# A combined high/low stationary operand for the 64-row sample tile in a feed-forward down projection

## The reference, cut to what matters

```python
h2 = _rms(x, P['norm_ffn_pre'])
u = jnp.square(jax.nn.relu(jnp.einsum('btd,df->btf', h2, P['w_up'])))      # 1024 -> 4096
x = x + _rms(jnp.einsum('btf,fd->btd', u, P['w_down']), P['norm_ffn_post'])  # 4096 -> 1024
```

## Time and profile before

| | |
|---|---|
| median of three runs | 2052.18 us (2047.31 to 2055.45) |
| profiled execution | 2048.07 us |
| its span in the trace | 2046.5 us |
| TensorE busy with matmuls | 1841.5 us, 90% |
| VectorE / ScalarE / GpSimd busy | 819.1 / 614.0 / 396.6 us |
| mean granted TensorE clock | 0.913 |

### The profile page before, as it was taken

The page is one execution under the profiler, slowest core; times in us unless marked ns, Lnnn a source line. Parts: engine busy times, 40 slices in busy tenths (PEclk is TensorE's granted clock), DMA queues, the critical chain, the costliest instruction groups (busy, mean ns, idle before and its releaser), DMA issues.

```text
span 2046.5 us, 33982 instructions
## 1 busy us (share of the span) xinstructions
PE 1841.5 (90%) x13899; PEld 1529.8 (75%) x13899; DVE 819.1 (40%) x1286; ACT 614.0 (30%) x1421; POOL 396.6 (19%) x606
## 2 busy tenths in 40 slices
PE   4999999999766798688887996999999999999996
PEld 4999999843545675577783445888888888999995
DVE  7111111265438673633321454333443333433336
ACT  3111111365446555322221222222222222222223
POOL 6400021387353556100010001000000000000004
PEclk9999999999777655688877997999999999999998
DMA  5111121200541001000004101111111111111102
GB/s 151 54 42 39 46 88 55 81 9 1 171 139 39 27 29 30 1 2 2 2 1 144 43 26 52 42 41 41 41 51 51 41 41 41 41 55 47 41 20 87
DMA packets 103829, 100.07 MB, mean 49 GB/s; under 512 B 15522, under 2 KB 89906, under 8 KB 103714
## 3 DMA queue, kind: packets, MB, share of 16 engines
q1 hardware_dynamic: 91266, 81.15, 13.4%
q0 software_dynamic: 6720, 17.11, 2.9%
q10 hardware_dynamic: 5728, 0.19, 0.2%
HBM read 85.78 MB, written 12.65 MB: 48 GB/s over the span
## 4 chain that ended last, share of the span: by engine, by line
PE 52%; DVE 4%; ACT 1%; issue 1%; DMA 0%; POOLq 0%; POOL 0%; DVEq 0%; SPq 0%
PE ps L416 12%; PE ps L417 12%; PE ps L418 12%; PE ps L2410 6%; PE ps L2055 1%; PE ps L1981 1%; DVE arena L2164 1%; DVE arena L2569 1%; PE ps L2076 1%; PE ps L2072 1%; PE ps L2108 0%; PE ps L2128 0%; PE ps L2097 0%; DVE h_split L2445 0%; PE ps L2126 0%
## 5 line engine op out<-in xcount | busy, mean ns | idle before, releaser
L416 PE MATMUL ps<-h_split,w_split 128*128 128x384 f32 (+1 forms) x768 | 251.5, 327 | 3.4 <-DVE w_split L2553 3.4
L418 PE MATMUL ps<-h_split,w_split 128*128 128x384 f32 (+1 forms) x768 | 251.4, 327 | 0.0
L417 PE MATMUL ps<-h_split,w_split 128*128 128x384 f32 (+1 forms) x768 | 251.3, 327 | 0.0
L2580 DVE TENSOR_TENSOR arena<-arena,ps 128x1024 f32<-128x1024 f32 x144 | 175.5, 1219 | 164.3 <-PE ps L418 164.3
L417 PE MATMUL ps<-w_split,u_split 128*128 128x512 f32 (+1 forms) x576 | 224.5, 390 | 0.0
L416 PE MATMUL ps<-w_split,u_split 128*128 128x512 f32 (+1 forms) x576 | 224.4, 390 | 0.0
L418 PE MATMUL ps<-w_split,u_split 128*128 128x512 f32 (+1 forms) x576 | 224.3, 389 | 0.0
L2602 POOL TENSOR_TENSOR arena<-arena 128x1024 f32<-128x1024 f32 (+1 forms) x9 | 23.3, 2593 | 774.7 <-DVE arena L2569 774.7
L2561 DVE TENSOR_TENSOR u_split<-above_u_split,u_split 128x384 fp32r<-128x384 f32 (+1 forms) x96 | 51.5, 537 | 298.3 <-ACT above_u_split L2534 298.3
L2513 ACT ACTIVATE w_split<-below_w_split 128x1024 fp32r<-128x1024 f32 x64 | 64.2, 1048 | 339.0 <-PE ps L418 321.7
L416 PEld LDWEIGHTS ps<-h_split,w_split 128*128 128x128 f32 x768 | 145.1, 189 | 5.1 <-issue 3.6
(11 more groups left out here) (380 smaller groups left out, 3507.3 us busy)
## 6 DMA issues: line engine op xcount, KB each, us to landing
below_w_split<-in_w_up SPq DMA_DIRECT2D x32, 512.0 KB, 4.8
below_w_split<-in_w_down SPq DMA_DIRECT2D x32, 512.0 KB, 3.9
w_raw<-in_w_in SPq DMA_DIRECT2D x27, 512.0 KB, 3.9
arena<-in_x_prompt SPq DMA_DIRECT2D x16, 512.0 KB, 3.8
arena<-in_cache_sb_k SPq DMA_DIRECT2D x64, 128.0 KB, 2.8
arena<-in_cache_sb_v POOLq DMA_DIRECT2D x64, 128.0 KB, 2.9
nat_scratch<-nat_stage POOLq DMA_DIRECT2D x32, 128.0 KB, 2.0
arena<-nat_scratch SPq DMA_DIRECT2D x16, 256.0 KB, 2.8
```

The source lines that it names most:

```text
L416: pe.matmul(out, w_hi, x_hi, start=first, stop=False)
L417: pe.matmul(out, w_hi, x_lo, start=False, stop=False)
L418: return pe.matmul(out, w_lo, x_hi, start=False, stop=last)
L2580: dve.tensor_tensor(y_acc[0:r, i, :], y_acc[0:r, i, :], p, ALU.add).then_inc(S("dn_out"), 1)
```

## The change

In the down projection the sample tile gets one stationary operand of 128 columns, the 64 high parts followed by the 64 low parts. Two matmuls per block and half, with the high and with the low part of w_down, take the place of three: 8 per chunk for this tile, not 12. The PSUM tile, and row tile 8 of `y_acc`, then hold the high rows' sums in partitions 0 to 63 and the low rows' in 64 to 127. For that `u_split` is laid out as [block, 2 x 1088], with the sample's low parts right behind its high parts; VectorE writes the low parts of the third group in two instructions, 256 and 64 columns. The term low x low is now included for the sample rows.

The sample tile moves from place 8 to place 6 of the down phase (DN_ORDER). After the last chunk the two halves of `y_acc`'s row tile 8 are added by two float32 matmuls, whose stationary operand `fold` (128 x 64, two identities on top of each other) VectorE builds at the end of its loop; VectorE copies the 64 x 1024 result from PSUM back into `y_acc`. VectorE's order at the end is now: finish tiles 0 to 5 behind the additions at places 1 to 6, nothing behind place 7, tile 6 behind place 8, then the copy, tile 7, tile 8.

```diff
@@ -2322,11 +2322,11 @@
             place.enter_context(nc.sbuf_tensor("below_h2_split", [P, NT * D], F32))
             h2_split = place.enter_context(nc.sbuf_tensor("h2_split", [P, 2, KD, TOK], F32R))
             place.enter_context(nc.sbuf_tensor("below_u_split", [P, NT * D], F32))
-            u_split = place.enter_context(nc.sbuf_tensor("u_split", [P, 2, FT, TOK], F32R))
+            u_split = place.enter_context(nc.sbuf_tensor("u_split", [P, FT, 2 * TOK], F32R))
             above_u = place.enter_context(nc.sbuf_tensor("above_u_split", [P, 2 * EG[0][1]], F32))
         up_hi, up_lo, dn_hi, dn_lo = (w_split[:, n, :, :] for n in range(4))
         h2_hi, h2_lo = h2_split[:, 0, :, :], h2_split[:, 1, :, :]
-        u_hi, u_lo = u_split[:, 0, :, :], u_split[:, 1, :, :]
+        u_hi, u_lo = u_split[:, :, 0:TOK], u_split[:, :, TOK + SMP:2 * TOK]
 
         w_raw = below_w[:, MIXER_CONSTS + P:MIXER_CONSTS + P + 2048].rearrange("p (g c) -> p g c", g=2)
         u_raw = above_u[:, :].rearrange("p (g c) -> p g c", g=2)
@@ -2468,6 +2468,8 @@
 
 
 
+        DN_ORDER = [0, 1, 2, 3, 4, 5, NT - 1, 6, 7]
+        fold = above_u[:, 0:SMP]
         NUP = 3 * FT
         UP_TILES = [(ft, tg) for tg in range(3) for ft in range(FT)]
 
@@ -2484,27 +2486,37 @@
                                     up_lo[:, ft, k * P:k * P + P], h2_hi[:, k, t0:t0 + tw],
                                     h2_lo[:, k, t0:t0 + tw], k == 0, k == KD - 1)
                     ins.then_inc(S("up_ps"), 1)
-                for i in range(NT):
-                    r = rows(i)
-                    if i == 0:
+                for pos, i in enumerate(DN_ORDER):
+                    if pos == 0:
                         pe.wait_ge(S("dn_split"), c * FT + FT)
-                    if i * P in [t0 for t0, _ in EG]:
-                        tg = [t0 for t0, _ in EG].index(i * P)
-                        pe.wait_ge(S("u_split"), c * NUP + FT * (tg + 1))
-                    if not first or i >= 3:
-                        pe.wait_ge(S("dn_out"), c * NT + (i - 1))
+                    if pos in (0, 3, 6):
+                        pe.wait_ge(S("u_split"), c * NUP + FT * (pos // 3 + 1))
+                    if not first or pos >= 3:
+                        pe.wait_ge(S("dn_out"), c * NT + (pos - 1))
                     for half in range(2):
                         cols = slice(half * 512, half * 512 + 512)
+                        out = ps[:, 2 + 2 * (pos % 3) + half, :]
                         for k in range(FT):
-                            x_hi, x_lo = (t[:, k, i * P:i * P + r] for t in (u_hi, u_lo))
-                            ins = three(pe, ps[0:r, 2 + 2 * (i % 3) + half, :], x_hi, x_lo, dn_hi[:, k, cols],
-                                        dn_lo[:, k, cols], k == 0, k == FT - 1)
+                            if i == NT - 1:
+                                both = u_split[:, k, T:T + 2 * SMP]
+                                pe.matmul(out, both, dn_hi[:, k, cols], start=(k == 0), stop=False)
+                                ins = pe.matmul(out, both, dn_lo[:, k, cols], start=False, stop=(k == FT - 1))
+                            else:
+                                x_hi, x_lo = (t[:, k, i * P:(i + 1) * P] for t in (u_hi, u_lo))
+                                ins = three(pe, out, x_hi, x_lo, dn_hi[:, k, cols], dn_lo[:, k, cols], k == 0,
+                                            k == FT - 1)
                     ins.then_inc(S("dn_ps"), 1)
             pe.wait_ge(S("hT"), 4 * NT)
             pe.wait_ge(S("m_x1"), NT)
             chunk(0, True)
             with pe.Fori(1, NCH) as c:
                 chunk(c, False)
+            pe.wait_ge(S("u_split"), NCH * NUP + 1)
+            pe.wait_ge(S("dn_out"), NCH * NT - 1)
+            for half in range(2):
+                ins = pe.matmul(ps[0:SMP, half, :], fold, y_acc[:, NT - 1, half * 512:half * 512 + 512], start=True,
+                                stop=True)
+            ins.then_inc(S("dn_ps"), 1)
 
         def mlp_act(act):
             def high(name, raw, hi, c, g, n):
@@ -2538,7 +2550,7 @@
             for i in range(NT):
                 r = rows(i)
                 s = d_ss[0:r, 2 * i:2 * i + 1]
-                act.wait_ge(S("dn_out"), (NCH - 1) * NT + i + 2)
+                act.wait_ge(S("dn_out"), (NCH - 1) * NT + DN_ORDER.index(i) + 2 if i < NT - 1 else NCH * NT + 2)
                 act.activation(end_junk[0:r, :], y_acc[0:r, i, :], ACT.Square, accum_out=s)\
                     .then_inc(*did("act"))
                 act.wait_ge(*so_far("act"))
@@ -2556,10 +2568,13 @@
             def low_u(c):
                 for q, (ft, tg) in enumerate(UP_TILES):
                     t0, tw = EG[tg]
-                    hi, lo = u_hi[:, ft, t0:t0 + tw], u_lo[:, ft, t0:t0 + tw]
+                    hi, raw, pw = u_hi[:, ft, t0:t0 + tw].bitcast(F32), u_raw[:, q % 2, :], min(tw, T - t0)
                     dve.wait_ge(S("up_out"), c * NUP + (q + 1))
-                    dve.tensor_tensor(lo, u_raw[:, q % 2, 0:tw], hi.bitcast(F32), ALU.subtract)\
-                        .then_inc(S("u_split"), 1)
+                    ins = dve.tensor_tensor(u_lo[:, ft, t0:t0 + pw], raw[:, 0:pw], hi[:, 0:pw], ALU.subtract)
+                    if pw < tw:
+                        ins = dve.tensor_tensor(u_split[:, ft, TOK:TOK + SMP], raw[:, pw:tw], hi[:, pw:tw],
+                                                ALU.subtract)
+                    ins.then_inc(S("u_split"), 1)
 
             def finish(i):
 
@@ -2571,13 +2586,13 @@
 
             def accumulate(n, tiles):
 
-                for i in tiles:
-                    r = rows(i)
-                    dve.wait_ge(S("dn_ps"), n * NT + (i + 1 - NT))
-                    if i == 0:
+                for pos in tiles:
+                    y = y_acc[:, DN_ORDER[pos], :]
+                    dve.wait_ge(S("dn_ps"), n * NT + (pos + 1 - NT))
+                    if pos == 0:
                         dve.wait_ge(S("dn_out"), n * NT + (1 - NT))
-                    p = ps[0:r, 2 + 2 * (i % 3):4 + 2 * (i % 3), :].rearrange("p a c -> p (a c)")
-                    dve.tensor_tensor(y_acc[0:r, i, :], y_acc[0:r, i, :], p, ALU.add).then_inc(S("dn_out"), 1)
+                    p = ps[:, 2 + 2 * (pos % 3):4 + 2 * (pos % 3), :].rearrange("p a c -> p (a c)")
+                    dve.tensor_tensor(y, y, p, ALU.add).then_inc(S("dn_out"), 1)
 
             low("up", w_raw, up_hi, up_lo, 0)
             low("dn", w_raw, dn_hi, dn_lo, 0)
@@ -2588,11 +2603,19 @@
                 accumulate(c, range(3, NT))
                 low("dn", w_raw, dn_hi, dn_lo, c)
                 low_u(c)
+            dve.wait_ge(S("u_split"), NCH * NUP)
+            dve.tensor_tensor(fold, ident[:, 0:SMP], ident[:, SMP:P], ALU.add).then_inc(S("u_split"), 1)
             dve.wait_ge(S("params"), 16 * (N_PAR_DMA + 2))
-            for i in range(NT):
-                accumulate(NCH, [i])
-                if i >= 1:
-                    finish(i - 1)
+            ended = 0
+            for pos in range(NT):
+                accumulate(NCH, [pos])
+                if 1 <= pos <= 6 or pos == 8:
+                    finish(ended)
+                    ended += 1
+            dve.wait_ge(S("dn_ps"), NCH * NT + 1)
+            dve.tensor_copy(y_acc[0:SMP, NT - 1, :], ps[0:SMP, 0:2, :].rearrange("p a c -> p (a c)"))\
+                .then_inc(S("dn_out"), 1)
+            finish(NT - 2)
             finish(NT - 1)
 
         def residual_gpsimd(pool):
```

## The result

The changed kernel takes 2035.59 us, the median of 15 runs (2030.47 to 2042.67), against 2048.84 us for the kernel before (15 runs, 2042.91 to 2055.45): 13.25 us less. The ratio is 0.9933 with a 95% interval of 0.9919 to 0.9947. The profiled execution took 2034.71 us, its span 2033.1 us, 13.4 us less than before.

The account below looks back on a forecast made before the run. TensorE's gapless feed-forward stream was taken as the bound: -14.2 us from 15 chunks and +0.7 us at the end give -13.5 us, from 2052.18 to 2038.7 us, range 2032.7 to 2044.7 us.

Parts of the forecast that it names:

- Bound: Feed-forward: TensorE's gapless stream alone sets the time, paid by distance between starts, 0.227 to 0.230 us per matmul.
- part 1: Sample tile, chunks 0 to 14: 8 matmuls for 12 save 0.94 us per chunk, 14.2 us in all.
- Rival (a): Sample tile: weight loads set the pace, so only 104 ns per chunk return, time 2051.3 us; chance 0.03.
- rival (d): Whole change: does not take effect as described, matmul for matmul; 2052 us plus 0.7 us; chance 0.02.
- Part 2: Waits within a chunk: about 3 us of slack remains and VectorE's extra 0.25 us twice a chunk is hidden; no cost.
- (b): Within chunks: saved time comes back as a wait for additions or weights; 2046.2 us at 0.5 us per chunk; chance 0.05.
- (c): Place 6: a wait there also costs the clock, at least 1.8 us lost per chunk, 2079 us; chance 0.02.
- Part 3: Last chunk and end: chunk 15's saving counts as nothing, fold and its building are hidden, end moves by +0.7 us.
- the last term: End of the kernel: tile 6 scaled 0.65 us late, GpSimd's addition beside the copy still 3.33 us; end +0.7 us.
- the lower bound that stood beside it: End of the kernel: if the copy does not hold GpSimd back, 3.33 us become 2.35 us; end moves -0.3 us.

Follow-up runs that it names:

- the eight narrow matmuls: Changed kernel with 8 matmuls of 64 stationary columns in the sample tile, low part of u, fold and copy left out: 2038.27 us (1 run), chunks 47.35 us.

## Why the prediction was right, and where it was not

**The sum.** -13.5 us and 2038.7 us were forecast; 13.25 us and 2035.59 us were measured. The 3.1 us between the two times are the base: the three runs of before that were shown have a median of 2052.18 us, and 15 have 2048.84 us, 3.3 us less. That the reduction came out within 0.3 us is in part luck. The interval of the ratio is one of 10.9 to 16.6 us, and the traces put the edit at 14.5 us, 1.0 us beyond the forecast.

**Bound and part 1: right.** The term was -15 x 0.944 = -14.2 us, and the traces give 0.94 + 13.25 = 14.2 us. What carried it was reading distances between starts rather than row durations: at 389 ns a row it would have been 23 us. The 131 ns of the Trainium skill ("TensorE: Matmul & The Clock Gate", section "Back-to-back issue gap") would have given 7.9 us; this case does not agree with it, since 4 and 36 wide matmuls fewer both give 0.227 us each. The change itself takes away 12 narrow ones and adds 8 wide ones, 0.946 us by 12 x 0.230 - 8 x 0.227 = 0.94 us. Rival (a), the weight loads, falls with the eight narrow matmuls, and rival (d) with the two groups of 64.

**Part 2: right.** The two low-part instructions take 0.43 + 0.22 us against 0.49 us, VectorE idles 2.96 us before them, and no wait of TensorE has appeared. That 3 us were in hand is borne out by the kernel without low weights, whose tiles all take 1.8 us. Rivals (b) and (c), wait and clock, did not occur.

**Part 3: chunk 15 right, the last term wrong in size.** The share of chunk 15 was counted as nothing, and the first addition comes 26.70 us after the chunk's start in both. Fold (1.93 us for 1.7 us), building (0.22 us for 0.30 us) and copy (1.21 us for 1.2 us) are off the path, which the kernel without them confirms. The delay of tile 6 was put at 0.65 us and is 0.66 us. The step that failed is "I take +0.7 us, since the row with the same shape in the same place shows the 3.33 us". Measured is -0.33 us, the lower bound that stood beside it. I had taken 64 x 1024 and the place for the cause; it was the 64-row addition, which the change does away with, and a copy of the same shape does not hold GpSimd. The Trainium skill's rule ("SBUF — State Buffer", section "SBUF: two separate sides"), by which a copy from PSUM takes no lock, gave the right sign and size here. The row of before goes against it: that addition has only one input in SBUF, too, and yet it holds GpSimd. Its other half is borne out by the kernel with sums in PSUM, where the scaling with one SBUF input falls from 2.5 us to 1.28 us beside GpSimd.

The error was 1 us in 13.5. With -0.3 us in place of +0.7 us the sum is the -14.5 us that the prediction gives beside its own, and that is the edit's worth in the traces.

## What to carry to other kernels

Where TensorE's stream has no gaps, an instruction taken out is worth the distance between starts, and a stationary operand that is half empty costs as much as a full one: filling it with a second part of the same rows takes a whole product away. Accumulate the halves separately through all chunks and fold once, somewhere that leaves other work for TensorE's clock and for the fold's result to hide behind. At a tail where VectorE and GpSimd take turns, keep one input of VectorE's instructions in PSUM, and let them cover all 128 rows.

## What the runs showed that was not expected

A VectorE addition of 64 x 1024 with one input in PSUM holds a GpSimd addition back by 1.0 us (3.33 and 3.36 us against 2.34 to 2.42 us), at both places tried; at 128 x 1024 it does not, nor does a 64 x 1024 copy from PSUM.

The fold's four TensorE instructions took 1.93 us behind a busy stream and 3.65 us after TensorE had idled 6.92 us, at a granted clock of 0.50. That, and not the order of the tiles, is most of what the fold costs at the last place.

The scatter between the traces does not come from the part under study, but for 1 us in chunk 0, which goes with a granted clock that rises later. Chunks 1 to 14 and the end repeat to 0.01 us in the two traces of the changed kernel, while the feed-forward starts anywhere from 1251.1 to 1264.8 us in the twelve profiled executions, behind code that is the same in all. Those 13.7 us are as large as the effect, and only the distances within the traces resolve single microseconds here.
